# A decoder block on one core: the first squares go to GpSimd, and TensorE's warm-up products become wider

## The chip, the core and the metric

The kernel runs on one core of a Trainium2 chip. The metric is device time in microseconds of the whole kernel; three runs of the kernel before gave 776.06, 776.08 and 776.13 us, median 776.08.

## The reference

The block takes x (512 tokens of 1024 features, float32). It computes an RMS norm, one wide projection, two token mixers that share it (sparse attention with a compressed, a selected and a window branch, and stick-breaking attention), gates that merge them, an output projection with a residual, then RMS norm, a squared-ReLU MLP with a residual, and a last RMS norm. What matters here is only the first line of it:

```python
def rmsnorm(x, g):
    xf = x.astype(jnp.float32)
    y = xf * lax.rsqrt(jnp.mean(xf * xf, axis=-1, keepdims=True) + EPS)
    return y * g.astype(jnp.float32)
...
        h = rmsnorm(x, norm_attn[layer])
        proj = h @ w_in[layer]
```

The kernel multiplies x*g with the weights first and scales by the inverse root (rstd) when a product leaves its bank. So the sum of squares is not needed for the first products, but for their evacuation.

## The kernel before

**Layout.** x lies transposed: eight tiles xs[:, k] of 128 features x 512 tokens. A weight panel is 8 x 128 x 128, 512 KB. Every float32 operand is split in two fp32r parts, high (the rounded value) and low (what rounding left), and a product is the sum of three: low weight x high input, high x low, high x high. In the code whi and wlo are the parts of a weight panel, hh and hl those of the scaled input.

**Who does what at the start.** Each engine runs its own program in order, and semaphores join them. SyncE and ScalarE issue the loads. ScalarE rounds: hh(k) for each input tile (line 725), the halves of panel 0 (716), panel 1 (702), the sparse value panels vw_h (730, 732). VectorE makes what is left: hl(k) (1027), wlo of panel 1 (1031), vw_l (1034, 1036). GpSimd makes wlo of panel 0 in two halves (667), and later the low parts of all panels (661). In the code all three kinds of low part are operations with two inputs in on-chip memory.

**Squares.** Behind that, ScalarE squares the eight input tiles into two alternating buffers (736), VectorE copies the first (1040) and adds the other seven (1043), ScalarE rounds the sum (739), VectorE takes the rest (1046), TensorE multiplies both with ones (1711), and ScalarE makes rstd by Ln (744) and Exp (746). Then it splits panels 4 and 5 (702), and the first two products leave their banks, scaled (1063).

**TensorE's order.** It is written out by hand. First 9 fp32 products of a 128x128 tile of ones with itself into bank 7, whose result nobody reads (1623). Then panel 0 and panel 1 as the parts come in: rounded (1630), weight_low (1634), input_low (1638) for panel 0; second_rounded (1642), second_input_low (1646) and the products with wlo (1675) for panel 1. The first six input tiles are taken for panel 0 alone (X_EARLY is 6), in the order rounded(i), weight_low(i-1), input_low(i-2). In code order weight_low(5), input_low(4) and input_low(5) then come ahead of six second_rounded. Behind both panels stand the sparse values, 0 and 1 (1686 to 1691), the product with ones (1711), the bias rows (1702), sparse values 2 and 3, and four transposes for rcol. Panels 4 and 5 follow (1600), then the hidden layer of the compressed tokens (1731), which needs the block matrices bm (1085) and their weights.

**Loads.** Four ring buffers hold panels; the load of panel p+4 waits until the products with the low part of panel p are done (w_used), so loads follow TensorE.

Of the kernel before, what the change touches and what calls it, by code (L numbers as in the profile page):

```python
# [30 lines left out]
ALU = mybir.AluOpType  # L31
ACT = mybir.ActivationFunctionType
AX = mybir.AxisListType

P = 128
T = 512
D = 1024
KT = D // P
RT = T // P
# [31 lines left out]
N_SEVEN = 1 + 4 * 3  # L71
NPANEL = P_FF + 64
X_EARLY = 6
WARM = 9

GM_IN_ATT = 12
GM_SB = 4
# [88 lines left out]
def slot(p):  # L166

    if p < P_FF + RING:
        return p % RING
    m = p - P_FF2  # L170
    return m % 2 if m < 24 else (2, 0, 1, 3)[m % 4]
# [15 lines left out]
def in_slot_ahead_of(p):  # L187

    if p < P_FF + RING:
        return panel_product(p - RING)  # L190
    m = p - P_FF2
    if m < 2:
        return "ff", 0, 4 + m
    if m < 24:
        return "f2", m - 2
    return (("wx", N_SEVEN - 1), ("f2", 22), ("f2", 23), ("wr", N_SEVEN - 1))[m - 24] if m < 28 else ("f2", m - 4)
# [34 lines left out]
def block_kernel(nc, xT, panels, w_gn, norms, rel_bias, pe, w1, b1, w2, onehot, cst, outT):  # L231
    with ExitStack() as ctx:
        top = [nc.sbuf_base + (-nc.sbuf_base) % 64]
# [3 lines left out]
        def place(name, shape, dt=F32, at=None):  # L237

            size = int(np.prod(shape[1:])) * (2 if dt == BF16 else 4)
            size += (-size) % 64  # L240
            start = top[0] if at is None else at
            if at is None:
                top[0] += size
            assert start + size <= limit, (name, start + size - limit)
            return nc.alloc_sbuf_tensor_at(name, shape, dt, offset=start)

        def sem(name):
            return ctx.enter_context(nc.semaphore(name))
# [10 lines left out]
        ones = place("ones", [P, P])  # L259
# [33 lines left out]
        negones = place("negones", [P, P], F32R)  # L293
        ident_r = place("ident_r", [P, P], F32R)
        diag_r = place("diag_r", [P, P], F32R)
        kn_lm = place("kn_lm", [P, G, T], F32R)
        rcol = place("rcol", [P, RT])
        gate = place("gate", [P, RT, H, 3])
# [13 lines left out]
        xs = place("xs", [P, KT, T], at=at_gm)  # L312
# [21 lines left out]
        sqt = place("sqt", [P, 2, T], at=at_sbq)  # L334
        sqs = place("sqs", [P, T], at=at_sbq + 4096)
# [17 lines left out]
        ones_r = place("ones_r", [P, P], F32R)  # L353
# [75 lines left out]
        bank = [ctx.enter_context(nc.psum_tensor(f"bank{i}", [P, T], F32)) for i in range(8)]  # L429
# [4 lines left out]
        def where(name):  # L434
            return name if isinstance(name, list) else USE[name]
# [11 lines left out]
        def result(eng, name):  # L447

            b, n = where(name)
            eng.wait_ge(full[b], n + 1)  # L450
            return bank[b]
# [10 lines left out]
        x_in = [sem(f"x_in{i}") for i in range(KT)]  # L462
# [6 lines left out]
        zero_done = sem("zero_halves")  # L469
        first_in, first_hi, first_lo = sem("first_half_panel_in"), sem("first_half_panel_hi"), sem("first_half_panel_lo")  # L470
        set_done, cast_done = sem("memsets"), sem("const_casts")
        h_hi, h_lo, sq_done, sqs_done = sem("h_hi"), sem("h_lo"), sem("sq_done"), sem("sqsum_done")
        table_hi, table_lo, sqs_hi, sqs_lo, x_ss_hi, x_ss_lo = sem("bias_table_hi"), sem("bias_table_lo"), sem("sqsum_hi"), sem("sqsum_lo"), sem("x_sqsum_hi"), sem("x_sqsum_lo")
        rst, gn_split, gate_st = sem("rstd_ready"), sem("gate_weights_split"), sem("branch_gate_steps")
# [27 lines left out]
        def landed(p):  # L502

            if p < P_FF + RING:
                return 16 * (p // RING + (1 if p < P_SV else 0))
            m = p - P_FF2
            if m < 0:
                return landed(p - 2) + 16
            if m < 24:
                return landed(P_FF + 4) + 16 * (m // 2 + 1)  # L510
            last = (landed_first(N_SEVEN - 1), landed(P_FF2 + 22), landed(P_FF2 + 23), landed(P_FF + 1))[m % 4]
            return last + 16 * ((m - 24) // 4 + 1)
# [141 lines left out]
        @block.gpsimd  # L654
        def _(pool):
            def low(p, i=0):

                s = slot(p)
                pool.wait_ge(w_hi, p + 1 + RING * i)
                for k in range(0, KT, 2):  # L660
                    ins = nc.gpsimd.tensor_tensor(wlo[:, s, k:k + 2], wraw[s][:, k:k + 2], whi[:, s, k:k + 2].bitcast(F32), ALU.subtract)  # L661
                ins.then_inc(w_lo, 1)


            for got, done, half in ((first_hi, first_lo, slice(0, 4)), (w_hi, w_lo, slice(4, 8))):
                pool.wait_ge(got, 1)
                nc.gpsimd.tensor_tensor(wlo[:, 0, half], wraw[0][:, half], whi[:, 0, half].bitcast(F32), ALU.subtract).then_inc(done, 1)
            for p in range(RING, P_SV):
                low(p)
            for c in range(RING):  # L670
                pool.wait_ge(w_hi, P_SV + c + 1)
                for k in range(0, KT, 2):
                    ins = nc.gpsimd.tensor_tensor(svw_l[:, c, k:k + 2], svraw[c][:, k:k + 2], svw_h[:, c, k:k + 2].bitcast(F32), ALU.subtract)
                ins.then_inc(w_lo, 1)
            rounds = (P_FF2 - P_SQK) // RING
            with pool.Fori(0, rounds) as i:
                for p in range(P_SQK, P_SQK + RING):
                    low(p, i)
            for p in range(P_SQK + RING * rounds, N_PLAIN):
                low(p)  # L680
# [3 lines left out]
        def _(act):  # L684
            A = nc.scalar.activation
# [10 lines left out]
            def split(p):  # L696

                s = slot(p)
                act.wait_ge(w_in[s], landed(p))
                if p >= RING:  # L700
                    result(act, in_slot_ahead_of(p))
                A(whi[:, s], wraw[s][:], ACT.Copy).then_inc(w_hi, 1)  # L702
# [27 lines left out]
                A(vw_h[:, :, P * c:P * c + P], wraw[P_V + c][:], ACT.Copy).then_inc(w_hi, 1)  # L730
            act.wait_ge(gn_in, 16)
            A(vw_h[:, :, 2 * P:VW], gns[:], ACT.Copy).then_inc(gn_split, 1)
            for k in range(KT):
                if k >= 2:
                    act.wait_ge(sqs_done, k - 1)
                A(sqt[:, k % 2], xs[:, k], ACT.Square).then_inc(sq_done, 1)

            act.wait_ge(sqs_done, KT)
            A(sqs_r[:, 0], sqs[:], ACT.Copy).then_inc(sqs_hi, 1)
            act.wait_ge(table_in, 16 * 3)  # L740
            A(oneh_r[:], oneh[:], ACT.Copy).then_inc(table_hi, 1)
            ps = result(act, "rms")
            act.wait_ge(set_done, 4)
            emptied(A(rstd_b[:], ps[:], ACT.Ln, bias=epsc[:], scale=1.0 / D), "rms")
            stored(act, "rms")
            A(rstd_b[:], rstd_b[:], ACT.Exp, scale=-0.5).then_inc(rst, 1)
            split(4)
            split(5)
            token_pairs(act, 0)

# [261 lines left out]
        def _(dve):  # L1012
            V = nc.vector
# [20 lines left out]
                V.tensor_tensor(vw_l[:, :, P * c:P * c + P], wraw[P_V + c][:], vw_h[:, :, P * c:P * c + P].bitcast(F32), ALU.subtract).then_inc(w_lo, 1)  # L1034
            dve.wait_ge(gn_split, 1)
            V.tensor_tensor(vw_l[:, :, 2 * P:VW], gns[:], vw_h[:, :, 2 * P:VW].bitcast(F32), ALU.subtract).then_inc(gn_split, 1)
            for k in range(KT):
                dve.wait_ge(sq_done, k + 1)
                if k == 0:
                    V.tensor_copy(sqs[:], sqt[:, 0]).then_inc(sqs_done, 1)  # L1040
                else:
                    dve.wait_ge(sqs_done, k)
                    V.tensor_tensor(sqs[:], sqs[:], sqt[:, k % 2], ALU.add).then_inc(sqs_done, 1)

            dve.wait_ge(sqs_hi, 1)
            V.tensor_tensor(sqs_r[:, 1], sqs[:], sqs_r[:, 0].bitcast(F32), ALU.subtract).then_inc(sqs_lo, 1)
# [525 lines left out]
        def _(pe_):  # L1572
            M = nc.tensor.matmul
# [44 lines left out]
                filled(ins, ("sv", r))  # L1618


            pe_.wait_ge(set_done, 1)
            for i in range(WARM):
                M(bank[7][:, 0:P], ones[:], ones[:], start=True, stop=True)

            b0, b1 = bank[USE[("pan", 0)][0]], bank[USE[("pan", 1)][0]]

            def rounded(k):
                pe_.wait_ge([first_hi, w_hi][k // 4], 1)
                pe_.wait_ge(h_hi, k + 1)
                M(b0[:], whi[:, 0, k, :], hh[:, k, :], start=(k == 0), stop=False)  # L1630

            def weight_low(k):
                pe_.wait_ge([first_lo, w_lo][k // 4], 1)
                return M(b0[:], wlo[:, 0, k, :], hh[:, k, :], start=False, stop=False)

            def input_low(i):
                pe_.wait_ge(h_lo, i + 1)
                return M(b0[:], whi[:, 0, i, :], hl[:, i, :], start=False, stop=(i == KT - 1))
# [8 lines left out]

            for i in range(X_EARLY):
                rounded(i)
                if i >= 1:  # L1650
                    weight_low(i - 1)
                if i >= 2:
                    input_low(i - 2)
# [94 lines left out]
            for m in range(2):  # L1748
                M(b[:, 0:64], w2k[:, m].rearrange("p a d -> p (a d)"), hidTk[:, m].rearrange("p g c -> p (g c)"),
                  start=(m == 0), stop=(m == 1))  # L1750
            for g in range(G):
                for m in range(2):
                    ins = M(b[:, 64 + 64 * g:128 + 64 * g],
                            hidTv[:, m, g].rearrange("p j c -> p (j c)"), w2v[:, m, :],
                            start=(m == 0), stop=(m == 1))
# [403 lines left out]
```

## Time and profile before

| | us |
|---|---|
| median of 3 runs | 776.08 |
| the profiled execution | 776.2 |
| its span | 774.4 |
| TensorE busy | 763.5 |
| VectorE busy | 509.6 |
| ScalarE busy | 395.9 |
| GpSimd busy | 274.2 |

The span runs from the first to the last instruction of the record; 1.8 us lie around it. Times in rows count from the span's start. PE is the row of products, PEld that of weight loads, DVE is VectorE, ACT ScalarE, POOL GpSimd, SP SyncE. Records of back-to-back products overlap: a product of 512 columns is recorded with about 0.39 us, but the next one begins 0.23 us after it. The mean granted clock over the span is 0.996.

### The profile page before, as it was taken

What the parts mean: (1) busy time and instruction counts of PE and PEld (TensorE: products, weight loads), DVE (VectorE), ACT (ScalarE), POOL (GpSimd) and SP (SyncE); (2) the same over time, 40 slices, a digit from 0 to 9 for tenths busy, and PEclk for the clock granted to TensorE, in tenths of its full rate; (3) what the DMA queues carried; (4) which work ended last, traced back from release to release, by engine and by line L of the source; (5) the groups of instructions that cost most, each with busy time, mean ns of one, the idle gap of its engine ahead of it and who ended that gap; (6) DMA issues with size and microseconds to landing.
All of it is one profiled execution on the core that took longest, in us unless ns stands there. A gap on an engine that the chain in (4) does not pass through costs nothing.

```text
span 774.4 us, 11317 instructions
## 1 busy us (share of the span) xinstructions
PE 763.5 (99%) x3964; PEld 631.7 (82%) x3964; DVE 509.6 (66%) x1047; ACT 395.9 (51%) x742; POOL 274.2 (35%) x358
## 2 busy tenths in 40 slices
PE   8999999999999999999999999999999999999996
PEld 6878888888877787778888888888888888888895
DVE  8546557787757676635444888778777777876334
ACT  6333324688956566565245665444444444443421
POOL 1255524511113332146556443333333322233630
PEclk9999999999999999999999999999999999999999
DMA  8964013210150111134322333322222333332213
GB/s 269 341 200 142 1 60 103 83 55 28 34 158 29 55 42 42 40 107 155 108 107 83 109 109 109 110 92 96 88 93 95 110 109 108 110 109 83 93 44 109
DMA packets 26004, 77.78 MB, mean 100 GB/s; under 512 B 3710, under 2 KB 6966, under 8 KB 25695
## 3 DMA queue, kind: packets, MB, share of 16 engines
q1 hardware_dynamic: 23868, 74.72, 29.4%
q10 hardware_dynamic: 2083, 2.37, 1.0%
q8 instruction: 31, 0.51, 0.3%
q14 instruction: 22, 0.18, 0.1%
HBM read 73.90 MB, written 2.13 MB: 98 GB/s over the span
## 4 chain that ended last, share of the span: by engine, by line
PE 92%; DVE 4%; ACT 2%; issue 1%; DMA 0%; POOL 0%; DVEq 0%; SPq 0%; ACTq 0%
PE bank L1600 29%; PE bank L2011 20%; PE bank L1983 11%; PE bank L1985 5%; PE bank L1917 2%; PE bank L1899 2%; PE bank L1831 2%; PE bank L1951 2%; PE bank L1956 2%; PE bank L1955 2%; PE bank L1876 2%; PE bank L1849 1%; PE bank L1612 1%; PE bank L1613 1%; PE bank L1614 1%
## 5 line engine op out<-in xcount | busy, mean ns | idle before, releaser
L661 POOL TENSOR_TENSOR wlo<-wraw,whi 128x256 fp32r<-128x256 f32 x336 | 259.3, 805 | 459.6 <-ACT whi L702 376.8
L702 ACT ACTIVATE whi<-wraw 128x1024 fp32r<-128x1024 f32 x75 | 78.6, 1054 | 26.4 <-PE bank L2011 16.2
L1600 PE MATMUL bank<-hh,wlo 128*128 128x512 f32 x304 | 81.1, 396 | 0.7 <-DVE gm L1245 0.5
L1600 PE MATMUL bank<-hl,whi 128*128 128x512 f32 x304 | 80.6, 392 | 0.0
L1600 PE MATMUL bank<-hh,whi 128*128 128x512 f32 x304 | 79.6, 391 | 0.0
L1600 PEld LDWEIGHTS bank<-hh,whi 128*128 128x128 f32 x304 | 56.6, 188 | 11.7
L1600 PEld LDWEIGHTS bank<-hl,whi 128*128 128x128 f32 x304 | 56.4, 188 | 11.8 <-issue 0.2
L1600 PEld LDWEIGHTS bank<-hh,wlo 128*128 128x128 f32 x304 | 55.4, 188 | 12.8 <-DVE gm L1245 0.9
L2011 PE MATMUL bank<-r_l,whi 128*128 128x512 f32 x224 | 57.9, 390 | 0.0
L2011 PE MATMUL bank<-r_h,wlo 128*128 128x512 f32 x224 | 56.3, 392 | 0.0
L2011 PE MATMUL bank<-r_h,whi 128*128 128x512 f32 x224 | 55.7, 389 | 0.0
L2011 PEld LDWEIGHTS bank<-r_h,whi 128*128 128x128 f32 x224 | 42.1, 188 | 8.9
L1307 DVE CUSTOM_DVE_ANT_0 ns<-bank,hank 128x128 f32<-128x128 f32 (+1 forms) x64 | 31.0, 485 | 25.7 <-PE bank L1882 20.9
L2011 PEld LDWEIGHTS bank<-r_l,whi 128*128 128x128 f32 x224 | 41.3, 188 | 7.9
L2011 PEld LDWEIGHTS bank<-r_h,wlo 128*128 128x128 f32 x224 | 40.5, 189 | 7.4
L875 ACT ACTIVATE ns<-ns,nmin 128x128 f32<-128x128 f32 (+1 forms) x64 | 35.7, 558 | 17.8 <-DVE nmin L1307 17.8
L1394 DVE TENSOR_TENSOR x_res<-bank,x_res 128x512 f32<-128x512 f32 x28 | 19.4, 691 | 32.4 <-PE bank L2011 32.4
L868 ACT ACTIVATE pt<-bank 128x128 f32<-128x128 f32 (+1 forms) x64 | 27.5, 431 | 25.7 <-PE bank L1899 25.7
L1983 PE MATMUL bank<-tt,sh 128*128 128x512 f32 x140 | 37.8, 392 | 0.2 <-DVE tmp L1381 0.2
L935 ACT ACTIVATE sh<-sr 128x512 fp32r<-128x512 f32 x44 | 25.1, 621 | 21.1 <-DVE sr L1415 21.1
L1316 DVE TENSOR_SCALAR ns<-ns,rec,gate 128x128 f32<-128x128 f32 (+1 forms) x64 | 31.4, 491 | 2.3
L1983 PE MATMUL bank<-h,whi 128*128 128x512 f32 x120 | 32.6, 393 | 0.0
(316 smaller groups left out, 1611.8 us busy)
## 6 DMA issues: line engine op xcount, KB each, us to landing
wraw<-in_panels SPq DMA_DIRECT2D x100, 512.0 KB, 3.3
land<-in_panels SPq DMA_DIRECT2D x13, 512.0 KB, 4.3
w1k<-in_w SPq DMA_DIRECT2D x1, 2048.0 KB, 9.2
w1v<-in_w SPq DMA_DIRECT2D x1, 2048.0 KB, 14.1
svraw<-in_panels SPq DMA_DIRECT2D x4, 512.0 KB, 5.2
hank<-bias_by_distance SPq DMA_DIRECT2D x4, 512.0 KB, 6.5
x_res<-in_xT SPq DMA_DIRECT2D x4, 512.0 KB, 4.5
out_dram<-x_res SPq DMA_DIRECT2D x12, 128.0 KB, 1.8
```

Source lines behind the costliest of these rows:

```text
L661: ins = nc.gpsimd.tensor_tensor(wlo[:, s, k:k + 2], wraw[s][:, k:k + 2], whi[:, s, k:k + 2].bitcast(F32), ALU.subtract)
L702: A(whi[:, s], wraw[s][:], ACT.Copy).then_inc(w_hi, 1)
L868: emptied(A(probs_tile(run, r), ps[:, 0:P * (r + 1)].rearrange("p (k t) -> p k t", k=r + 1), ACT.Copy), ("t", u))
L875: A(ns[i % 4][:, 0:n], ns[i % 4][:, 0:n], ACT.Exp, scale=-1.0, bias=nmin[:, i % 4:i % 4 + 1], accum_out=rsum[:, i % 4:i % 4 + 1]).then_inc ...
L935: A(sum_hi(j, i), sum_raw(j, i), ACT.Copy).then_inc(s_hi, 1)
L1307: emptied(V.tensor_tensor_reduce(ns[i % 4][:, 0:n], ps[:, 0:n], hank[:, p, g, 0:n][:, ::-1], 1.0, 3.0e38, ALU.add, ALU.min, nmin[:, i % 4: ...
L1316: V.tensor_scalar(ns[u % 4][:, 0:n], ns[u % 4][:, 0:n], rec[:, u % 4:u % 4 + 1], gate[:, r, g * HG + p, 2 - br:3 - br], ALU.mult, ALU.mult ...
L1394: emptied(V.tensor_tensor(x_res[:, n], ps[:], x_res[:, n], ALU.add), name)
L1600: ins = M(b[:, cols], lhs, (xl if a == 1 else xh)[:, row + k, cols], start=(m == 0), stop=(m == 23))
L1983: M(o[:], wh[:, k], x[:, :, k], start=(start and k == 0), stop=False, skip_group_check=True)
L1985: ins = M(o[:, 0:T // 2], wl[:, k], x[:, 0, k], start=False, stop=(stop and k == 3), skip_group_check=True)
L2011: ins = M(b[:], (wlo if a == 0 else whi)[:, s, k, :], (r_l if a == 1 else r_h)[:, q % 2 * 8 + k], start=(i == 0), stop=(i == 23))
```

## The change

Three things. GpSimd squares input tiles 0, 1 and 2 and adds them up in a buffer of its own, behind its two half panels; ScalarE squares only tiles 3 to 7, and VectorE adds these five to GpSimd's sum (so it has no copy, and two adds fewer). The products of ones become ten instead of nine, with the rounded ones and 512 columns (fp32r, one 128x128 tile read four times), they wait for the cast of ones, and one more stands behind rounded(0) and one behind rounded(1). And ScalarE splits panel 4 ahead of Ln instead of behind Exp.

```diff
-WARM = 9
+WARM = 10
+X_POOL = 3
...
+        sq_pool = place("sq_pool", [P, 2, T], at=top[0])
...
@@ gpsimd, behind the two halves of panel 0
+            for k in range(X_POOL):
+                pool.wait_ge(x_in[k], 16)
+                if k >= 2:
+                    pool.wait_ge(pool_sq, 2 * k - 1)
+                nc.gpsimd.tensor_tensor(sq_pool[:, min(k, 1)], xs[:, k], xs[:, k], ALU.mult).then_inc(pool_sq, 1)
+                if k:
+                    pool.wait_ge(pool_sq, 2 * k)
+                    nc.gpsimd.tensor_tensor(sq_pool[:, 0], sq_pool[:, 0], sq_pool[:, 1], ALU.add).then_inc(pool_sq, 1)
@@ scalar
-            for k in range(KT):
+            for k in range(KT - X_POOL):
                 if k >= 2:
                     act.wait_ge(sqs_done, k - 1)
-                A(sqt[:, k % 2], xs[:, k], ACT.Square).then_inc(sq_done, 1)
-
-            act.wait_ge(sqs_done, KT)
+                A(sqt[:, k % 2], xs[:, X_POOL + k], ACT.Square).then_inc(sq_done, 1)
+
+            act.wait_ge(sqs_done, KT - X_POOL)
             A(sqs_r[:, 0], sqs[:], ACT.Copy).then_inc(sqs_hi, 1)
             act.wait_ge(table_in, 16 * 3)
             A(oneh_r[:], oneh[:], ACT.Copy).then_inc(table_hi, 1)
+            split(4)
             ps = result(act, "rms")
...
             A(rstd_b[:], rstd_b[:], ACT.Exp, scale=-0.5).then_inc(rst, 1)
-            split(4)
             split(5)
@@ vector
-            for k in range(KT):
+            dve.wait_ge(pool_sq, 2 * X_POOL - 1)
+            for k in range(KT - X_POOL):
                 dve.wait_ge(sq_done, k + 1)
-                if k == 0:
-                    V.tensor_copy(sqs[:], sqt[:, 0]).then_inc(sqs_done, 1)
-                else:
+                if k:
                     dve.wait_ge(sqs_done, k)
-                    V.tensor_tensor(sqs[:], sqs[:], sqt[:, k % 2], ALU.add).then_inc(sqs_done, 1)
+                V.tensor_tensor(sqs[:], sqs[:] if k else sq_pool[:, 0], sqt[:, k % 2], ALU.add).then_inc(sqs_done, 1)
@@ tensor
-            pe_.wait_ge(set_done, 1)
+            def product_of_ones(copies):
+                M(bank[7][:, 0:P * copies], ones_r[:], ones_r[:].unsqueeze(1).to_broadcast([P, copies, P]), start=True, stop=True)
+
+            pe_.wait_ge(set_done, 5)
             for i in range(WARM):
-                M(bank[7][:, 0:P], ones[:], ones[:], start=True, stop=True)
+                product_of_ones(RT)
...
             for i in range(X_EARLY):
                 rounded(i)
+                if i < 2:
+                    product_of_ones(RT)
```

## Rows read from the trace of the kernel before

**Rows 1.** The page: busy time by engine; costliest groups (xcount | busy us, mean ns | idle).

```profile
PE 763.5 (99%) x3964; PEld 631.7 (82%) x3964; DVE 509.6 (66%) x1047; ACT 395.9 (51%) x742; POOL 274.2 (35%) x358
...
L1600 PEld LDWEIGHTS bank<-hh,whi 128*128 128x128 f32 x304 | 56.6, 188 | 11.7
```

**Rows 2.** Waits of TensorE from 50 us on, the longest (us in total, times, longest).

```profile
PE bank L2067 <- ACT fin_sq L1000: 0.5, 1, 0.5
```

**Rows 3.** TensorE: the warm-up's durations (ns min/median/max), then the timeline (start, us).

```profile
L1623 PEld LDWEIGHTS bank<-ones x18: 192/333/338, 1.1 to 4.5; 128*128 128x128 f32 x18
L1623 PE MATMUL bank<-ones x18: 274/421/579, 1.1 to 4.6; 128*128 128x128 f32 x18
...
5.75 0.50 PE L1630 MATMUL bank<-hh,whi 128*128 128x512 f32 x1 [0.87 <-ACT whi L716]
...
7.66 0.75 PE L1634 MATMUL bank<-hh,wlo 128*128 128x512 f32 x1 [0.73 <-POOL wlo L667]
...
13.04 1.52 PE L1642 MATMUL bank<-hh,whi 128*128 128x512 f32 x6
...
17.80 1.98 PE L1675 MATMUL bank<-hh,wlo 128*128 128x512 f32 x8
...
26.02 0.63 PE L1711 MATMUL bank<-sqs_r,ones_r 128*128 128x512 f32 x2
```

**Rows 4.** Windows: length, busy us of PE, PEld, DVE, ACT, POOL; granted clock; DMA, GB/s.

```profile
4.88:7.66 2.78, 0.98 (x3) 0.38 (x3) 2.78 (x3) 1.60 (x3) 1.83 (x1) 1.00 1.04 383
...
7.74:11.15 3.41, 3.41 (x8) 2.54 (x9) 3.03 (x5) 3.03 (x6) 1.33 (x1) 0.50 1.05 414
...
765.43:768.84 3.41, 1.97 (x11) 1.16 (x10) 0.42 (x1) 1.26 (x3) 0.00 (x0) 1.00 0.00 0
768.84:772.26 3.42, 0.00 (x0) 0.00 (x0) 3.26 (x8) 0.05 (x1) 0.00 (x0) 1.00 0.56 187
```

**Rows 5.** ScalarE's timeline: the split of panel 1.

```profile
10.77 1.06 ACT L702 ACTIVATE whi<-wraw 128x1024 fp32r<-128x1024 f32 x1 [0.38 <-DMA wraw<-in_panels]
```

**Rows 6.** VectorE's timeline, the first 25 us.

```profile
5.86 0.62 DVE L1027 SCALAR_TENSOR_TENSOR hl<-xs,nrm,hh 128x512 fp32r<-128x512 f32 x1
6.40 1.75 DVE L1027 SCALAR_TENSOR_TENSOR hl<-xs,nrm,hh 128x512 fp32r<-128x512 f32 x1
...
9.19 1.31 DVE L1027 SCALAR_TENSOR_TENSOR hl<-xs,nrm,hh 128x512 fp32r<-128x512 f32 x1 [0.38 <-ACT hh L725]
...
13.80 1.22 DVE L1031 TENSOR_TENSOR wlo<-wraw,whi 128x1024 fp32r<-128x1024 f32 x1
...
17.21 0.35 DVE L1036 TENSOR_TENSOR vw_l<-gns,vw_h 128x192 fp32r<-128x192 f32 x1
...
18.00 5.47 DVE L1043 TENSOR_TENSOR sqs<-sqs,sqt 128x512 f32<-128x512 f32 x7
24.17 0.69 DVE L1046 TENSOR_TENSOR sqs_r<-sqs,sqs_r 128x512 fp32r<-128x512 f32 x1 [0.70 <-ACT sqs_r L739]
```

**Rows 7.** GpSimd's timeline, the first 25 us.

```profile
5.78 1.83 POOL L667 TENSOR_TENSOR wlo<-wraw,whi 128x512 fp32r<-128x512 f32 x1 [5.32 <-ACT whi L716]
8.62 1.33 POOL L667 TENSOR_TENSOR wlo<-wraw,whi 128x512 fp32r<-128x512 f32 x1 [1.02 <-ACT whi L716]
```

**Rows 8.** Timelines of VectorE and GpSimd at 434 to 438 us.

```profile
434.67 1.22 DVE L1368 TENSOR_TENSOR x_ss_r<-mx,x_ss_r 128x512 fp32r<-128x512 f32 x1
435.31 1.18 POOL L661 TENSOR_TENSOR wlo<-wraw,whi 128x256 fp32r<-128x256 f32 x1
435.82 1.75 DVE L1370 TENSOR_TENSOR tr<-h2raw,tr 128x1024 f32<-128x1024 f32 x1
```

**Rows 9.** DMA issues from 17.0 to 19.7 us: KB each, median us to landing.

```profile
wraw<-in_panels SPq DMA_DIRECT2D x1, 512.0 KB, 3.2
```

**Rows 10.** Timelines of VectorE and TensorE around the block matrices.

```profile
41.99 1.98 DVE L1085 TENSOR_TENSOR bm<-x,pes 128x496 f32<-128x496 f32 x2 [0.17 <-DMA x<-ckv]
...
45.60 0.43 PE L1731 MATMUL bank<-w1k,bm 128*64 128x256 f32 x1
```

More of the change, by code:

```diff
@@ L471, in block_kernel @@
         set_done, cast_done = sem("memsets"), sem("const_casts")
+        pool_sq = sem("gpsimd_squares_and_sums")
         h_hi, h_lo, sq_done, sqs_done = sem("h_hi"), sem("h_lo"), sem("sq_done"), sem("sqsum_done")
```

## The prediction

> **What bounds the kernel now.** The page comes first: TensorE is busy for 763.5 of 774.4 us [rows 1]. The reader is to see that nothing but TensorE's own order of work sets the time. Next the waits of TensorE from 50 us on: the longest is 0.5 us [rows 2], and there are four, 1.4 us together. So a microsecond that TensorE gains or loses at the start comes out at the end nearly whole, and the change touches only the start. I then read the first 27 us engine by engine.
>
> TensorE [rows 3]: 9 fp32 products of ones (18 pieces), the first real product at 5.75, then, after a wait for GpSimd's low half, an unbroken stream from 7.66. The windows [rows 4] say what the clock did: 2.78 us with 0.98 us of TensorE work, then 3.41 us at 0.50 of the clock with 8 products (0.43 us each). At full clock a product of 512 columns takes 0.227 us: 21 of them lie between the first product of the second panel (13.04) and the products with that panel's low half (17.80) [rows 3]. A fully used full clock would have saved half of 3.41 us, 1.7 us. That is what the products of ones are after.
>
> **The products of ones.** The clock column shows 1.00 from the start, but the warm-up says otherwise: its weight loads take 333 ns in the median and 192 ns at best [rows 3], where a load of this shape takes 188 ns in the long run [rows 1]. So TensorE begins at half clock and comes to full near the end of the warm-up, about 4.3 us. The new products start one cast later, near 1.45 us instead of 1.06. At 0.43 us each about 6.7 go before 4.3, and 3.3 at 0.227 end near 5.1. Were all at half clock, the ten would end at 5.75, just when the first real product can start. Either way they delay nothing. The two inside the stream go into time in which TensorE is idle today: of the 2.78 us from 4.88 to 7.66 it is busy for 0.98 [rows 4], and both fit there even at 0.43 us each, so they cost nothing.
> Do they hold the clock? Before the fall at 7.74 TensorE had stood idle for 1.8 of 2.78 us. With the change it works some 0.2 us longer at the front and 0.5 us more between the real products, so it idles 1.1 us. At the kernel's end it was idle for 1.44 of 3.41 us and the clock was still 1.00 in the stretch behind that [rows 4]. So I take it that the clock holds past 7.74. The Trainium skill (TensorE: Matmul & The Clock Gate, section "Why this matters for your kernels") asks only that no long idle gap stands between bursts; by it the clock would not have fallen in the kernel before, where the longest gap is about 1 us. The trace disagrees, and decides.
>
> What can a held clock give? At full clock TensorE runs into its inputs: input_low(5) needs the sixth hl of VectorE (end 11.83), and the first product of the second panel needs ScalarE's split, which ends at 10.77+1.06 = 11.83 [rows 5]. It would start at 12.10 instead of 13.04: a gain of 0.94 us at most.
>
> **GpSimd's five operations.** This is the part that decides. GpSimd is idle after its second half panel at 8.62+1.33 = 9.95 [rows 7], so the work looks free; but VectorE has its two-input operations just there: hl 3 to 7, wlo of panel 1, vw_l. And these two engines do not run such operations side by side. [Rows 6, 7]: hl0 ran 5.86 to 6.48; GpSimd's operation, issued at 5.78, took 1.83 us where the next took 1.33, and ended at 7.61, that is 1.13 us after hl0; hl1, issued at 6.40, ended at 8.15, 0.54 after GpSimd. hl3, issued at 9.19 under the second one, ended at 10.50, 0.55 after 9.95. At 434 to 438 us, where both have a queue, they strictly take turns [rows 8]: VectorE ends 435.89, GpSimd (256 elements) 436.49, that is +0.60, VectorE (1024 elements) 437.57, +1.08. So each turn costs: VectorE 512 elements 0.55, 1024 elements 1.08, GpSimd 512 elements 1.13.
>
> Square and add on GpSimd are not in the trace. Bounds from the rows: 0.60 (as its 256 elements) to 1.33 (the whole duration of a 512-element one, taken alone). I take 1.13, the row of the same shape under the same contention. The three squares and two adds then take turns with VectorE from the end of hl3:
> 10.50; square 11.63; hl4 12.18; square 13.31; hl5 13.86; add 14.99; hl6 15.53; square 16.66; hl7 17.21; add 18.34; wlo of panel 1 19.42; then vw_l, without turns, 2.54 us later as now (15.02 to 17.56), at 21.96.
> In short: wlo ends at 13.77+5h for a turn h of GpSimd. It ended at 15.02 before, so VectorE loses 4.4 us.
>
> TensorE: it waits at input_low(5) until 13.90 (11.60+2h, plus the semaphore), does that product and 21 more (22 x 0.227 = 5.0, plus about 0.1 for a pipeline that starts empty) by about 18.95, then waits for wlo until 19.47. That stood at 17.80; with 0.11 us for the empty pipeline (at 7.66 a product after a wait added that much) the loss is **1.78 us**. The clock saved before 11.15 is wholly eaten by these two waits: with or without it TensorE stands at 13.90. The sparse values then start at 21.6, and need vw_l after eight products, at 22.6: 21.96 is in time.
>
> **Sum of squares.** Gone are a copy and two adds on VectorE and three squares on ScalarE. VectorE's five adds follow at 21.9 with the present pitch, 0.78 (seven in 5.47) [rows 6], and end near 25.8; ScalarE's rounding and VectorE's low part end 1.39 us later (24.17+0.69 against 18.00+5.47), at 27.2. TensorE comes to the product that uses them at 26.02+1.78 = 27.8 [rows 3]: 0.6 us to spare. The POOL wait stands in VectorE's queue behind vw_l and costs nothing, since the last add is done at 18.34; it holds only these adds.
>
> **split(4) ahead of Ln.** Panel 4 lands 3.2 us after an issue at 17.09 [rows 9]; now about 1 us later, near 21.4. The split (1.06 us) runs after the one-hot cast, 27.3 to 28.4, and Ln can start at 27.8+0.66: covered, 0 to 0.1 us. Without cover it would cost rstd 1.06 us. GpSimd's low(4) waits for this split, and its own five operations ended 9 us earlier. All DMA issues of this stage follow TensorE's progress, so they shift with it. The block matrices end at 43.97, TensorE's use starts at 45.60 [rows 10]: 1.6 us of slack that both ends keep.
>
> Sum: the profiled execution has 776.2 us (span 774.4, 1.8 around it), and +1.78 gives 778.0; the median of the runs is 0.1 lower, so the forecast is **777.9 us**.
>
> **Rivals.**
> A second fall of the clock. If the clock holds at 7.74, TensorE gets early to the waits for hl4 and hl5: from 11.45 to 13.90 it then does one product and idles 2.2 us, more than the 1.8 us ahead of the fall in the kernel before [rows 4]. A fall that lasts as long as that one (7.74 to 11.15) costs 1.7 us; 0.5 of it lies in the wait for wlo, so +1.2: 779.1 us. For it: that idle time. Against it: work stands densely on both sides of it, from 7.66 to 11.45 and from 13.90 on. By the cited rule of the Trainium skill on gaps it doesn't happen, and the time stays 777.9.
> The added products don't hold the clock at 7.74. Then TensorE is at input_low(4) at 12.59 as now, waits until 13.86 all the same, and the time is again 777.9; the change does not do what it says, at no price.
> Not slower: GpSimd's operations leave VectorE alone, or are short. One mechanism, the turn h at hl5 and wlo: without blocking, 0.94 us are gained, 775.2. At h = 0.60 hl5 ends at 12.80 and TensorE is as late as today, 776.1. It decides from h = 0.80, where wlo (13.77+4.0) meets 17.80. For it: no square or add of GpSimd is in the trace. Against it: four places with the turns to 0.05 us. At the other bound, h = 1.33, wlo ends at 20.4: 778.9.
>
> **Chances.** Forecast 0.50 (own range 777.4 to 778.3, from 1.05 to 1.2 us per turn and the small terms), second fall 0.27, clock not held 0.10 (777.9), cheap or unblocked GpSimd 0.13. Least change that can be told is about 0.2%, 1.55 us: bounds 774.5 and 777.6. Faster 0.04: it needs more than the 0.94 us that the inputs allow. Slower: about seven tenths of the forecast and of the third case, nearly all of the second: 0.68. Same: 0.28. Range 776.6 to 779.2; outside it lie most of the last rival and the edge of the second.
>
> **What would show it.** hl4 and hl5 ending near 12.2 and 13.9, GpSimd's five operations at 1.6 to 1.8 us each, wlo of panel 1 at 19.4, TensorE waiting twice, granted clock 1.00 from 7.74 to 11.15, and the sums' product at 27.8. Wrong, if hl5 still ends near 11.8, if wlo is ready before TensorE needs it, or if the shift at the end is not the one at 28 us.

## The result, and the profile after

| | median us | runs | lowest to highest |
|---|---|---|---|
| the kernel before | 776.55 | 22 | 775.8 to 778.33 |
| the changed kernel | 777.49 | 22 | 777.33 to 778.02 |

The ratio is 1.0013, 95% interval 1.0007 to 1.0018: 0.94 us slower by the medians, 0.13%. So the change costs a little, less than the 1.8 us forecast, and less than the 0.2% that the prediction set as its bound for "slower". The two profiled executions differ by more: span 775.7 against 774.4 us. The time lies 0.4 us from the forecast of 777.9, but the difference was forecast at twice its size; the account at the end says how the two go together.

A first thing to see is in the table itself: the kernel before spreads over 2.5 us, the changed one over 0.7. The three runs that the prediction started from (776.06 to 776.13) showed nothing of that.

VectorE and GpSimd of the changed kernel, from their timelines (start us, duration; merged rows have a count). It answers to [rows 6, 7]:

```profile
10.53 1.52 DVE L1038 SCALAR_TENSOR_TENSOR hl<-xs,nrm,hh 128x512 fp32r<-128x512 f32 x1
11.97 1.52 DVE L1038 SCALAR_TENSOR_TENSOR hl<-xs,nrm,hh 128x512 fp32r<-128x512 f32 x1
13.42 1.78 DVE L1038 SCALAR_TENSOR_TENSOR hl<-xs,nrm,hh 128x512 fp32r<-128x512 f32 x1
...
16.57 2.32 DVE L1042 TENSOR_TENSOR wlo<-wraw,whi 128x1024 fp32r<-128x1024 f32 x1
...
21.08 0.35 DVE L1047 TENSOR_TENSOR vw_l<-gns,vw_h 128x192 fp32r<-128x192 f32 x1
...
25.91 0.69 DVE L1056 TENSOR_TENSOR sqs_r<-sqs,sqs_r 128x512 fp32r<-128x512 f32 x1 [0.70 <-ACT sqs_r L750]
```

```profile
10.01 2.94 POOL L675 TENSOR_TENSOR sq_pool<-xs 128x512 f32<-128x512 f32 x2
13.03 1.62 POOL L678 TENSOR_TENSOR sq_pool<-sq_pool 128x512 f32<-128x512 f32 x1
14.80 1.30 POOL L675 TENSOR_TENSOR sq_pool<-xs 128x512 f32<-128x512 f32 x1
16.18 1.63 POOL L678 TENSOR_TENSOR sq_pool<-sq_pool 128x512 f32<-128x512 f32 x1
```

Read the ends, not the durations. hl4 is issued at 10.53 and ends at 12.05, hl5 at 13.50, hl6 at 15.20, and wlo of panel 1, which took 1.22 us in [rows 6], is recorded with 2.32 and ends at 18.89. The recorded time holds a wait: each stood for one operation of GpSimd. GpSimd's too: five operations, 1.30 to 1.63 us each, and each ends 0.90 us (a square) or 1.15 us (an add) behind the end of one of VectorE's.

TensorE's timeline, with what it waited for in brackets, and the windows (as in [rows 4]):

```profile
1.49 4.08 PE L1632 MATMUL bank<-ones_r 128*128 128x512 f32 x10 [1.49 <-DVE ones_r L1029]
6.06 0.50 PE L1643 MATMUL bank<-hh,whi 128*128 128x512 f32 x1 [0.49 <-ACT whi L727]
...
12.10 0.49 PE L1651 MATMUL bank<-hl,whi 128*128 128x512 f32 x1
13.55 0.50 PE L1651 MATMUL bank<-hl,whi 128*128 128x512 f32 x1 [0.95 <-DVE hl L1038]
13.89 1.55 PE L1655 MATMUL bank<-hh,whi 128*128 128x512 f32 x6
...
18.94 2.11 PE L1690 MATMUL bank<-hh,wlo 128*128 128x512 f32 x8
...
27.29 0.63 PE L1726 MATMUL bank<-sqs_r,ones_r 128*128 128x512 f32 x2
```

```profile
4.88:7.66 2.78, 2.09 (x7) 0.79 (x6) 2.61 (x3) 1.50 (x3) 1.54 (x1) 1.00 1.04 396
7.74:11.15 3.41, 3.11 (x12) 2.06 (x13) 3.02 (x4) 2.75 (x5) 2.42 (x2) 1.00 1.05 412
```

The clock is 1.00 where it was 0.50, and TensorE does 12 products in the stretch in which it did 8. It has no use of them: it waits for hl5 until 13.55, starts panel 1 at 13.89 (13.04 before), reaches wlo at 18.94 (17.80) and the product of the sums at 27.29 (26.02). That is 1.27 us, and the spans differ by 1.3.

### The profile page after: what moved, and what is told of

Its sections match the earlier page's. It is cut to its first block, busy times and chain, and to the rows that moved or that the text cites. A ratio compares the mean times of both kernels' runs of the same rounds, so it can differ in the third digit from the quotient of the medians.

```text
span 775.7 us, 11303 instructions
## 1 busy us (share of the span) xinstructions
PE 763.9 (98%) x3958; PEld 629.9 (81%) x3958; DVE 512.2 (66%) x1044; ACT 394.4 (51%) x739; POOL 281.6 (36%) x363
## 4 chain that ended last, share of the span: by engine, by line
PE 90%; DVE 5%; ACT 2%; issue 1%; DMA 1%; DVEq 0%; ACTq 0%
PE bank L1610 29%; PE bank L2026 20%; PE bank L1998 11%; PE bank L2000 5%; PE bank L1932 2%; PE bank L1914 2%; PE bank L1846 2%; PE bank L1966 2%; PE bank L1970 2%; PE bank L1971 2%; PE bank L1891 1%; PE bank L1864 1%; PE bank L1622 1%; PE bank L1623 1%; PE bank L1624 1%
```

## The experiments

All ratios are against runs of the kernel before on the same chip; they are worked out from all the runs and are not the quotient of two medians. There were three such chips, with 776.84 us for the kernel before beside e1 to e4, 776.93 beside e5 to e8 and 776.61 beside e9 and e10, so a median is best compared within one of these groups. e6 has six runs, e10 one, the others eleven or twelve. "hl5", "wlo" and "sums" are, from each profiled execution, the ends of hl5 and of panel 1's wlo and the start of the product of the sums.

| | products of ones | GpSimd | median us | ratio, 95% | hl5 | wlo | sums |
|---|---|---|---|---|---|---|---|
| before | 9 narrow | - | 776.55 | 1 | 11.83 | 15.02 | 26.02 |
| changed | 10 wide + 2 | 3 squares, 2 adds | 777.49 | 1.0013 (1.0007 to 1.0018) | 13.50 | 18.89 | 27.29 |
| e1 | 10 wide + 2 | - | 775.77 | 0.9987 (0.9978 to 0.9996) | 12.13 | 15.61 | 25.59 |
| e2 | 9 narrow | 3 squares, 2 adds | 778.18 | 1.0012 (1.0004 to 1.0021) | 15.11 | 20.49 | 28.87 |
| e3 | 10 wide + 2 | 1 square | 776.41 | 0.9993 (0.9985 to 1.0002) | 12.97 | 15.54 | 26.37 |
| e4 | 10 wide + 2 | 5 memsets | 776.01 | 0.9983 (0.9975 to 0.9992) | 12.71 | 16.22 | 26.20 |
| e5 | 10 wide + 2 | 2 squares, 1 add | 777.29 | 1.0003 (0.9993 to 1.0014) | 13.46 | 16.96 | 26.85 |
| e6 | 10 wide + 2 | as changed, later | 780.62 | 1.0044 (1.003 to 1.0057) | 12.00 | 15.41 | 28.78 |
| e7 | 10 wide | - | 775.77 | 0.9988 (0.9979 to 0.9997) | 12.13 | 15.57 | 25.56 |
| e8 | 10 wide + 2 | - (split(4) early) | 775.86 | 0.9985 (0.9976 to 0.9993) | 11.85 | 14.89 | 25.24 |
| e9 | 11 narrow | - | 776.89 | 0.9998 (0.9988 to 1.0007) | 12.58 | 15.75 | 28.09 |
| e10 | 9 narrow | - | 777.76 (one run) | | 12.86 | 16.12 | 27.55 |

### The two halves of the change, each alone (e1, e2)

e1 is the kernel before with this; e2 is the changed kernel without it, and with split(4) back behind Exp:

```diff
-WARM = 9
+WARM = 10
...
-            pe_.wait_ge(set_done, 1)
+            pe_.wait_ge(set_done, 5)
             for i in range(WARM):
-                M(bank[7][:, 0:P], ones[:], ones[:], start=True, stop=True)
+                product_of_ones(RT)
...
                 rounded(i)
+                if i < 2:
+                    product_of_ones(RT)
```

> The kernel before with the twelve wide products of ones alone; squares, sums and split(4) stay as they were. Theory 'turns' (the loss comes from VectorE and GpSimd taking turns on two-input operations): with GpSimd idle behind 10 us, the sixth hl ends near 11.9 and wlo of panel 1 near 15.1, the granted clock is 1.00 from 4.9 to 770, the first product of panel 1 starts at 12.1 to 12.5 instead of 13.04, and the product of the sums at 25.1 to 25.5 instead of 26.02: 0.5 to 0.9 us faster than the kernel before, ratio 0.9988 to 0.9994. Rival 'warm-up' (the wide products themselves delay the first real ones, or take more than they give): not faster than before, 1.000 to 1.0013.

> The kernel before with the squares and sums of three tiles on GpSimd alone; the nine fp32 products of ones and split(4) stay as they were. Theory 'turns': hl 5 near 13.5, wlo near 18.9, product of the sums near 27.3, whether the clock falls at first or not, because TensorE waits at hl 5 either way: as the changed kernel, 1.0010 to 1.0018 against the kernel before. Rival 'warm-up': without the wide products the loss is gone, 0.9995 to 1.0003.

e1: ratio 0.9987, just past the end of the range of "turns" and far from that of "warm-up". Panel 1 starts at 12.52. hl5 and wlo keep VectorE's own pace in its timeline:

```profile
11.39 0.74 DVE L1027 SCALAR_TENSOR_TENSOR hl<-xs,nrm,hh 128x512 fp32r<-128x512 f32 x1
...
14.39 1.22 DVE L1031 TENSOR_TENSOR wlo<-wraw,whi 128x1024 fp32r<-128x1024 f32 x1
```

e2: 1.0012, the loss of the changed kernel without its products of ones. In its profiled execution hl5 is later still (15.11, expected 13.5). The cause lies ahead of the squares: input tile 2 came late, and ScalarE waited 2.56 us for it. TensorE was at half clock for 6.82 us besides:

```profile
9.01 0.72 ACT L736 ACTIVATE hh<-xs,nrm 128x512 fp32r<-128x512 f32 x1 [2.56 <-DMA xs<-in_xT]
```

```profile
8.14:14.96 6.82, 5.11 (x13) 4.01 (x13) 4.83 (x5) 5.51 (x9) 4.55 (x4) 0.50 1.05 374
```

This execution (779.03 us) is the slowest of e2's twelve. VectorE takes its turns in it (an hl of 1.52 us, wlo of 2.31), but TensorE comes so late that it waits neither for hl5 (ready at 15.11, taken at 15.29) nor for wlo (20.49 and 20.55). That e2 loses rests on its runs, not on this trace.

So the wide products gain, GpSimd's work loses, and "warm-up" falls in both runs.

### How many turns (e3, e5)

```diff
-X_POOL = 3
+X_POOL = 1
```

and the same with 2.

> The changed kernel with one tile squared by GpSimd instead of three, so one operation of GpSimd (a turn of 0.90 us) instead of five (2.7 + 2.3 us). Theory 'turns': hl 4 ends near 12.0, hl 5 near 12.7, wlo near 16.0, before TensorE wants it; 22 products from 12.75 end near 17.8 and the time is that of the kernel before or up to 0.3 us less: ratio 0.9995 to 1.0003. Rival 'warm-up': as the changed kernel, 1.0010 to 1.0015.

> The changed kernel with two tiles on GpSimd: two squares and one add instead of three and two. Theory 'turns': three turns, so hl 4 and hl 5 end as in the changed kernel (12.0 and 13.5), wlo two turns earlier (near 16.9 instead of 18.9), before TensorE wants it. TensorE's first wait stays, the second goes: 22 products from 13.55 end near 18.65 where 17.80 stood before; the sums' product at about 26.9. About 0.3 us faster than the changed kernel, ratio to the kernel before 1.0003 to 1.0010, between one square and three. Rival: the loss goes with GpSimd's total work, two thirds of the changed kernel's.

e3 on VectorE, GpSimd and TensorE; hl4 stands for the one square, hl5 does not. Its ratio, 0.9993, is a little below the range expected:

```profile
10.79 1.52 DVE L1038 SCALAR_TENSOR_TENSOR hl<-xs,nrm,hh 128x512 fp32r<-128x512 f32 x1
...
12.23 0.74 DVE L1038 SCALAR_TENSOR_TENSOR hl<-xs,nrm,hh 128x512 fp32r<-128x512 f32 x1
```

```profile
10.28 1.49 POOL L675 TENSOR_TENSOR sq_pool<-xs 128x512 f32<-128x512 f32 x1
```

```profile
13.03 0.50 PE L1651 MATMUL bank<-hl,whi 128*128 128x512 f32 x1 [0.16 <-DVE hl L1038]
```

e5 waits for hl5 as long as the changed kernel does (0.95 us there), and no more for wlo, which ends at 16.96, before TensorE is there:

```profile
13.51 0.50 PE L1651 MATMUL bank<-hl,whi 128*128 128x512 f32 x1 [0.94 <-DVE hl L1038]
```

The medians are 775.8 (no square), 776.4 (one), 777.3 (two) and 777.5 (three). The steps are not in proportion to GpSimd's work (1, 3 and 5 operations). The first two squares stand ahead of hl5 and the first add behind it; on one chip they cost 1.5 us together (e5 against e7). The last square and add stand ahead of hl7 and wlo, where TensorE has time left, and cost 0.2. That is the form that "turns" gives.

The traces give the same order, but other steps. The spans are 774.0, 774.7, 775.2 and 775.7, and the product of the sums starts at 25.59, 26.37, 26.85 and 27.29. By them the three operations of e5 cost 1.2 us and the last two 0.4 to 0.5. The rival of e5 (two thirds of a loss of 1.7 us, so 1.1) is therefore not excluded by the times. What speaks against it is where TensorE waits: for hl5 as long as in the changed kernel, and no more for wlo.

### Is it work, or reading? (e4)

```diff
-                nc.gpsimd.tensor_tensor(sq_pool[:, min(k, 1)], xs[:, k], xs[:, k], ALU.mult).then_inc(pool_sq, 1)
+                nc.gpsimd.memset(sq_pool[:, min(k, 1)], 1.0).then_inc(pool_sq, 1)
...
-                    nc.gpsimd.tensor_tensor(sq_pool[:, 0], sq_pool[:, 0], sq_pool[:, 1], ALU.add).then_inc(pool_sq, 1)
+                    nc.gpsimd.memset(sq_pool[:, 0], 1.0).then_inc(pool_sq, 1)
```

> The changed kernel with GpSimd's five operations replaced by memsets of the same tiles; it leaves out the squares of tiles 0 to 2 (the sum starts from ones). They write on-chip memory and read none. If the turns are for reading, hl and wlo keep the pace of the kernel before (hl 5 near 11.9, wlo near 15.1) and the time is 0.5 to 1.0 us below the kernel before, ratio 0.9987 to 0.9994. Rival 'any work of GpSimd blocks VectorE's two-input operations': each memset costs VectorE its own length, hl 5 ends behind 12.5, wlo behind 16.5, and the ratio is 1.000 or more.

VectorE and GpSimd in e4, from 11 to 13 us:

```profile
11.31 0.74 DVE L1038 SCALAR_TENSOR_TENSOR hl<-xs,nrm,hh 128x512 fp32r<-128x512 f32 x1
...
11.97 0.74 DVE L1038 SCALAR_TENSOR_TENSOR hl<-xs,nrm,hh 128x512 fp32r<-128x512 f32 x1
```

```profile
11.24 0.53 POOL L675 MEMSET sq_pool<- 128x512 f32 x1
...
12.47 0.53 POOL L675 MEMSET sq_pool<- 128x512 f32 x1
```

Both memsets run at the same time as an hl, and each hl keeps its 0.74 us (wlo its 1.22). The whole is at 0.9983, as fast as without any work of GpSimd within the intervals. So it is not that GpSimd works, nor the semaphores, but that both engines read. (Whether an operation of GpSimd that reads a single tile takes a turn too was not run.) The Trainium skill (SBUF — State Buffer, section "Who interferes with whom") says that a VectorE instruction with two inputs in on-chip memory contends with a GpSimd instruction that reads it, and not with one that only writes; this trace agrees. The profiled execution had hl5 at 12.71, 0.9 us later than in the kernel before and past the 12.5 of the rival. That hangs on a late input and not on GpSimd: ScalarE took up tile 2 at 8.19, where it was 7.30 in the kernel before, and TensorE waited 0.74 us for it.

```profile
8.19 0.72 ACT L736 ACTIVATE hh<-xs,nrm 128x512 fp32r<-128x512 f32 x1 [1.38 <-DMA xs<-in_xT]
```

### The same work at another place (e6)

```diff
+            pool.wait_ge(w_lo, 2)
             for k in range(X_POOL):
```

> The changed kernel, but GpSimd starts its squares only when wlo of panel 1 is done (w_lo at 2). Theory 'turns': hl and wlo as in the kernel with the products of ones alone (hl 5 near 12.0, wlo near 15.4), TensorE's waits at hl 5 and wlo are gone; the turns now fall on vw_l and put off the end of the sum: squares and adds end near 22.9, VectorE's five adds near 26.9, its low part near 28.2, and TensorE, early at 25.3, waits there until 28.2. So the loss returns as a wait of about 2.9 us at the product of the sums: ratio 1.0010 to 1.0035. Rival 'only hl and wlo matter': sums' product at 25.3, ratio 0.9988.

hl5 and wlo are clean (12.00, 15.41), the rival is out, and the wait stands at the product that was expected, until 28.78 instead of 28.2 and 3.24 us long instead of 2.9. But the ratio is 1.0044, more than the range given. TensorE and then the windows:

```profile
28.78 0.70 PE L1727 MATMUL bank<-sqs_r,ones_r 128*128 128x512 f32 x2 [3.24 <-DVE sqs_r L1057]
```

```profile
25.54:28.78 3.24, 0.00 (x0) 0.03 (x1) 2.30 (x6) 2.13 (x4) 0.00 (x0) 1.00 1.04 440
29.88:33.29 3.41, 3.41 (x15) 3.31 (x15) 1.97 (x3) 2.08 (x3) 3.41 (x5) 0.50 0.94 387
```

A wait of 3.24 us, and behind it 3.41 us at half clock, worth 1.7 us: 4.9 us together, and 780.62 less the 775.77 of e7, on the same chip, is 4.85. The expectation had priced the wait and not what an idle TensorE loses behind it.

This run also shows what GpSimd's operations take when VectorE stands idle (it waited 3.73 us for the sum until 23.37):

```profile
20.93 1.04 POOL L676 TENSOR_TENSOR sq_pool<-xs 128x512 f32<-128x512 f32 x1
22.05 1.29 POOL L679 TENSOR_TENSOR sq_pool<-sq_pool 128x512 f32<-128x512 f32 x1
```

A turn of 0.90 us for a square and 1.15 for an add is thus the whole operation but 0.14 us. For VectorE it is 0.55 of 0.74 and 1.08 of 1.22.

### What holds the clock (e7, e9, e10)

e7 is e1 without the two products between the real ones, e9 the kernel before with WARM at 11, e10 the kernel before, traced once more.

> The kernel before with ten wide products of ones at the start and none between the first real products. If the two in between are needed to hold the clock, it falls in most executions (clock of a run 0.993 to 0.997, times spread from 775.5 to 778.5 as in the kernel before): ratio near 1.000. If the ten are enough, times stay as close together as with all twelve, near 0.9987.

> The kernel before with eleven fp32 products of ones of 128 columns instead of nine, nothing else. They take about 4.7 us at half clock and reach to 5.7 instead of 4.9. If it counts that TensorE has no idle time ahead of the first real product, the clock holds in nearly all executions and the time is that of the ten wide ones, ratio 0.9985 to 0.9992. If the wide, rounded products are what holds it, the clock falls as in the kernel before: 0.9996 to 1.0004.

> The kernel before, unchanged, for a second trace of it. Expected: the same order of work; where the clock falls, or whether it falls, may differ from the first trace (which had it at half from 7.74 to 11.15), and with it the time within 775.5 to 778.8.

e7 is as fast as e1, and nine of its eleven runs lie between 775.4 and 775.9 us; the two inner products give nothing that can be told. The eleven narrow ones give nothing either (0.9998), and their runs spread as those of the kernel before. The first products in the traces of e7, e9 and e10:

```profile
1.48 4.63 PE L1622 MATMUL bank<-ones_r 128*128 128x512 f32 x10 [1.48 <-DVE ones_r L1018]
5.93 1.47 PE L1633 MATMUL bank<-hh,whi 128*128 128x512 f32 x2
```

```profile
1.06 4.32 PE L1623 MATMUL bank<-ones 128*128 128x128 f32 x22 [1.06 <-DVE onec L1015]
6.10 0.50 PE L1630 MATMUL bank<-hh,whi 128*128 128x512 f32 x1 [0.72 <-ACT whi L716]
```

```profile
1.06 4.21 PE L1623 MATMUL bank<-ones 128*128 128x128 f32 x18 [1.06 <-DVE onec L1015]
6.23 1.47 PE L1630 MATMUL bank<-hh,whi 128*128 128x512 f32 x2 [0.96 <-ACT whi L716]
...
12.33 0.63 PE L1634 MATMUL bank<-hh,wlo 128*128 128x512 f32 x1
12.75 0.60 PE L1638 MATMUL bank<-hl,whi 128*128 128x512 f32 x1
13.18 0.40 PE L1630 MATMUL bank<-hh,whi 128*128 128x512 f32 x1
```

In e7 no idle time stands ahead of the first real product. In e9 0.72 us stands there: the clock had come to full at about 4.4, so the narrow products ended early, and then it fell for 6.8 us. In e10 the products keep a pitch of 0.43 us until 13.2, and none of the narrow ones was faster than 0.42, so TensorE was at half clock from the start on; the first trace of the same kernel had it full from about 4.3 and at half only from 7.74 to 11.15. What the clock does at the start differs from one execution of the kernel before to the next. The Trainium skill (TensorE: Matmul & The Clock Gate, Part 1) says that where the change comes varies from run to run; these traces agree.

The time differs with it: the runs of the kernel before with a mean clock of 0.998 took 775.4 to 776.1 us, those with 0.993 778.0 to 778.8. Those with 0.997, as e10, took anything from 776.2 to 778.1, since the clock's column does not show a half clock that holds from the start. But the clock is not all that differs. In e10 tile 2 came late (ScalarE took it up at 8.34, not 7.30), so that the third input tile's product started at 9.20 instead of 8.20. Of the 1.53 us by which panel 1 starts later (14.57 against 13.04), 1.0 had arisen there, and the rest came at half clock. How the two share the spread of the runs without a trace is open.

What it is in the wide products that holds the clock is not settled by these runs: their width, their kind, or that in e7 they reach to the first real product. e9 changed neither width nor kind and still left a gap. A short gap alone does not decide it: the changed kernel had 0.49 us there, e3 and e6 0.34, and in their traces the clock did not fall at the start; they have the two inner products as well.

### split(4) (e8)

```diff
             A(oneh_r[:], oneh[:], ACT.Copy).then_inc(table_hi, 1)
+            split(4)
             ps = result(act, "rms")
...
-            split(4)
             split(5)
```

> The kernel with the twelve products of ones and split(4) ahead of Ln, squares as before. Expected: ScalarE is idle between the one-hot cast and Ln for 0.7 us in the kernel with the products of ones alone, and the split takes 1.05, so Ln comes 0.3 to 0.4 us later; TensorE does not wait for rstd there, since four transposes behind two more sparse values need it first, so the ratio is that of the products of ones alone, 0.9984 to 0.9990. Rival: the split delays rstd and so the block matrices; then TensorE waits at the hidden layer (45.3) and the ratio is 0.9990 or more.

0.9985, that of the products of ones alone. ScalarE's timeline:

```profile
24.86 1.04 ACT L702 ACTIVATE whi<-wraw 128x1024 fp32r<-128x1024 f32 x1
25.91 0.69 ACT L745 ACTIVATE rstd_b<-bank,epsc 128x512 f32<-128x512 f32 x1
```

The product of the sums starts at 25.24, and Ln follows it by 0.67 us, as before (26.02 and 26.68 there): the split fits into the wait, and the delay of 0.3 to 0.4 us that was expected did not come. e8 is the changed kernel without GpSimd's part, so the difference is what the five operations cost: 777.49 - 775.86 = 1.6 us by the medians, 2.0 when each is taken against its own kernel before (0.94 above it, 1.07 below it), and 2.1 by the spans (775.7 and 773.6). Of all versions e1, e7 and e8 are the fastest and the same within what can be told: they beat the kernel before by 0.12 to 0.15%, and the changed one by more.

## Why the prediction came out as it did, step by step

- **The turns: right.** Place, order and form as forecast; e4 shows that it is reading, e1 and e8 that nothing else of the change costs, e6 that the price only moves when the work moves.
- **Size of a turn: too large by a fifth for the squares.** Taken: 1.13 us for each of five. Measured in the changed kernel: 0.90 for each of the three squares (10.60 to 11.50), 1.15 for the two adds. Squares and subtraction have the same shape, but a square reads one tile twice, and it is shorter even without contention (1.04 us in e6); that the one causes the other is not shown. With h at 0.90 and 1.15 the chain 13.77 + 2.7 + 2.3 gives 18.8; measured 18.89, forecast 19.42. This is the term of the sum that was mis-sized: 0.5 us.
- **TensorE's two waits: right.** For hl5 until 13.55 (forecast 13.90), for wlo until 18.94 (19.47). Loss at the product of the sums 1.27 us instead of 1.78, and it went to the end of the span undiminished (1.3).
- **The base: not one number.** The three runs shown lay within 0.07 us, the trace had one course of the clock; 22 runs have a median 0.5 us higher. Against those the span's 1.3 us become 0.94. The prediction called the effect of the clock nothing ("with or without it TensorE stands at 13.90"). For the changed kernel that is nearly so: e2, without wide products, loses as much against its kernel before (1.0012) as the changed kernel does (1.0013). For the kernel before it was wrong: its executions lie up to 3.3 us apart (775.45 to 778.79), with the clock and with the landing of the inputs. The gain of the ones was thus left out of the base.
- **Luck in the number.** The loss was forecast at 1.78 us and is 0.94; the base was taken as 776.08 and is 776.55. The first was too high by 0.84, the second too low by 0.47, and so 777.9 lies only 0.4 us from 777.49. The mechanism was right; that the time fits so well is in part chance.
- **The clock held past 7.74: right** in the trace, with less idle time than forecast (0.7 of 2.78 us, not 1.1). The second fall did not come in it, although TensorE did one product between 11.97 and 13.55, and none of the 22 runs is near its price of 779.1 (the slowest took 778.02). Other versions with wide products were not as steady: e1 has a run with a mean clock of 0.994 (777.37 us), e5 one with 0.993 (780.77 us). They were not traced.
- **At most 0.94 us to gain without turns: right against the traced execution.** e1 starts panel 1 at 12.52 and its span is 0.4 us shorter, e8 at 12.24 with 0.8. By the medians both gain 1.1 us, more than the bound, since the median of the kernel before holds its slower courses too; its fastest runs (775.45 us beside e1, 775.58 beside e8) are as fast as theirs (775.40, 775.44).
- **Sum of squares and split(4): right.** Sums' low part ready at 26.60, TensorE there at 27.29: 0.7 us to spare, forecast 0.6.
- **The chances.** "Slower by more than 0.2%" had 0.68, and it came out 0.13% slower, which is the case that had 0.28. The forecast stood only 0.3 us behind that bound, so a turn of 0.90 instead of 1.13 and the base were enough to cross it.

## What to carry to other kernels

An engine that stands idle is free only if what it would read does not go over a path that the busy engine needs: look at the durations of the two engines' operations where they already overlap, and price the new work in turns on the operation that the critical engine waits for next. Work moved off a path costs where its turn falls, not by its amount: here 1.2 to 1.5 us for the operations around hl5, and 0.2 to 0.5 for a square and an add further back. And take the spread of the kernel before from more than three runs before a change of a microsecond is judged by it; the ten wide products of ones were worth 1 us by the medians, which three runs and one trace of the kernel before did not show. They narrowed the spread in some versions (e8 0.6 us, e3 0.7), less in e7 (1.5) and e1 (2.1).

## What the runs showed of the hardware beyond that

- A square of one 128x512 float32 tile on GpSimd has a turn of 0.90 us, an add or subtraction of two tiles 1.15 and 1.13, which for square and add is all but 0.14 us of what they take alone; a memset of the same tile takes 0.53 and takes no turn from VectorE.
- The clock column reads 1.00 ahead of the first change that it records: in e10 up to 13.18 us, while the products' pitch of 0.43 us tells half clock. At the start of a trace go by the pitch.
- 3.24 us of waiting cost 4.9: the wait and then a stretch at half clock (e6).
- Input loads land up to 2.3 us apart between executions of the same order of issues: ScalarE took up tile 2 at 6.70 in e8, at 7.30 in the kernel before and at 9.01 in e2.
